# VectorE sums the squares of seven blocks for three RMS norms, and the ones product of TensorE takes that sum and the eighth block

## What is computed

```python
def rmsnorm(x, g):
    xf = x.astype(jnp.float32)
    y = xf * lax.rsqrt(jnp.mean(xf * xf, axis=-1, keepdims=True) + RMS_EPS)
    return (y * g.astype(jnp.float32)).astype(x.dtype)
...
            x = x + mix
            x = x + swiglu(rmsnorm(x, p['norm_ffn_even'][i]), p['ffn_w_gate'][i], p['ffn_w_up'][i], p['ffn_w_down'][i])
        else:
            mix, cb = conformer_conv(rmsnorm(x, p['norm_mix_odd'][i]), conf_bufs[i], p, i)
            new_conf_buf.append(cb)
            x = x + mix
            x = x + moe_swiglu(rmsnorm(x, p['norm_ffn_odd'][i]), p['moe_router'][i], p['moe_w_gate'][i],
                               p['moe_w_up'][i], p['moe_w_down'][i])
```

## Time and profile before

| | |
|---|---|
| median of 3 runs | 1404.65 us |
| lowest, highest | 1401.75 us, 1405.23 us |
| the profiled execution | 1402.96 us |
| its span, first to last instruction | 1401.2 us |
| mean granted clock of TensorE | 0.988 |
| TensorE busy | 1351.3 us (96%) |
| VectorE busy | 363.2 us (26%) |
| ScalarE busy | 178.7 us (13%) |
| GpSimd busy | 61.9 us (4%) |

### The profile page before, as it was taken

The page is one execution under the profiler, slowest core; times in us unless marked ns, Lnnn a source line. Parts: engine busy times, 40 slices in busy tenths (PEclk is TensorE's granted clock), DMA queues, the critical chain, the costliest instruction groups (busy, mean ns, idle before and its releaser), DMA issues.

```text
span 1401.2 us, 18234 instructions
## 1 busy us (share of the span) xinstructions
PE 1351.3 (96%) x7743; PEld 868.3 (62%) x7743; DVE 363.2 (26%) x807; ACT 178.7 (13%) x376; POOL 61.9 (4%) x87
## 2 busy tenths in 40 slices
PE   7999998999999999989999999999999999999976
PEld 6888887888888888758755544434343443444432
DVE  3536885221111006922300020201111011011102
ACT  1231423010001001041200000000000100100002
POOL 2004110000001002000000000000000000000000
PEclk9999999999999999999999999999999999999998
DMA  8538622574547233410899999999999999999994
GB/s 265 202 123 275 222 91 91 180 208 127 174 144 230 77 120 120 128 43 16 314 399 403 401 397 399 394 403 400 398 399 391 403 393 404 387 374 405 391 403 197
DMA packets 169667, 381.49 MB, mean 272 GB/s; under 512 B 7661, under 2 KB 63517, under 8 KB 169531
## 3 DMA queue, kind: packets, MB, share of 16 engines
q1 hardware_dynamic: 161571, 358.96, 69.2%
q0 software_dynamic: 3184, 11.40, 2.6%
q10 hardware_dynamic: 4834, 9.99, 2.2%
HBM read 372.41 MB, written 9.01 MB: 272 GB/s over the span
## 4 chain that ended last, share of the span: by engine, by line
PE 87%; DVE 6%; DMA 4%; SPq 1%; ACT 1%; issue 1%; ACTq 0%; DVEq 0%
PE ps L1703 29%; PE ps L2166 14%; PE ps L2231 12%; PE ps L2181 8%; PE ps L2191 4%; DVE region L1407 3%; PE ps L1921 3%; PE ps L2242 2%; PE ps L1712 2%; DMA region<-in_moe_w_gate_dram 2%; DMA big<-in_moe_w_down_dram 1%; PE ps L2123 1%; PE ps L2085 1%; DMA big<-in_w_in_even_dram 1%; PE ps L2208 1%
## 5 line engine op out<-in xcount | busy, mean ns | idle before, releaser
L1703 PE MATMUL ps<-big 128*128 128x264 f32 x1376 | 311.9, 388 | 2.3 <-DMA big<-in_w_in_even_dram 2.3
L1703 PEld LDWEIGHTS ps<-big 128*128 128x128 f32 x1376 | 262.1, 191 | 48.2 <-DMA big<-in_w_in_even_dram 2.5
L2166 PE MATMUL ps<-big,region 128*64 128x384 f32 (+3 forms) x1200 | 217.7, 459 | 7.6 <-DMA big<-in_moe_w_up_dram 4.6
L2166 PEld LDWEIGHTS ps<-big,region 128*64 128x64 f32 (+1 forms) x1200 | 115.4, 147 | 105.4 <-issue 61.5
L1703 PE MATMUL ps<-region,big 128*128 128x264 f32 x704 | 162.4, 391 | 3.7 <-ACT region L965 3.7
L2231 PE MATMUL ps<-big,region 128*64 128x512 f32 (+1 forms) x608 | 156.1, 604 | 2.2 <-DMA big<-in_moe_w_down_dram 1.6
L1703 PEld LDWEIGHTS ps<-region,big 128*128 128x128 f32 x704 | 135.2, 193 | 27.6 <-issue 4.1
L2181 PE MATMUL ps<-big,region 128*64 128x384 f32 (+1 forms) x720 | 111.0, 460 | 0.0
L2231 PEld LDWEIGHTS ps<-big,region 128*64 128x64 f32 (+1 forms) x608 | 50.1, 144 | 93.7 <-issue 90.0
L2181 PEld LDWEIGHTS ps<-big,region 128*64 128x64 f32 x720 | 51.3, 137 | 56.6 <-issue 49.0
L1618 DVE TENSOR_TENSOR region<-region,ps 128x384 f32<-128x384 f32 (+1 forms) x24 | 12.2, 520 | 227.0 <-PE ps L2166 227.0
(11 more groups left out here) (366 smaller groups left out, 1048.9 us busy)
## 6 DMA issues: line engine op xcount, KB each, us to landing
big<-in_moe_w_up_dram SPq DMA_DIRECT2D x48, 1536.0 KB
big<-in_moe_w_gate_dram SPq DMA_DIRECT2D x40, 1536.0 KB
big<-in_moe_w_down_dram SPq DMA_DIRECT2D x40, 1536.0 KB
big<-in_w_in_even_dram SPq DMA_DIRECT2D x10, 2048.0 KB
big<-in_moe_w_gate_dram SPq DMA_DIRECT2D x16, 1024.0 KB
big<-in_moe_w_up_dram SPq DMA_DIRECT2D x16, 1024.0 KB
big<-in_moe_w_down_dram SPq DMA_DIRECT2D x16, 1024.0 KB
region<-in_moe_w_gate_dram SPq DMA_DIRECT2D x8, 1536.0 KB
```

The lines of the kernel that those rows point to most:

```text
L1703: ins = mm(ps[:, 0:T], w[:, c, cols:cols + P], src[:, c, :], start=c == 0, stop=c == nk - 1)
L2166: ins = mm(out, xg[:, 4 * j + c, 0:cap], w[:, c, r, :], start=j + c == 0, stop=j + c == 4)
```

## The change

VectorE gets six adds per norm. Ahead of residual c, for c from 2 to 7, it waits until block c - 1 has been squared, and adds it to block 0 of `SQ2`. So block 0 ends as the sum of blocks 0 to 6. TensorE's products with ones behind the `wo`, `fd` and `w2` tiles are taken out. In place of the last one stands `stat_two`, with two products: the sum, and block 7.

```diff
             def residual(k, name, bias=None, gain=None):
 
                 for c in range(DC):
+                    if c >= 2:
+                        dve.wait_ge(sem("sq_ready"), 8 * (k + 1) + c)
+                        reach()
+                        ins = v.tensor_tensor(SQ2[:, 0, :], SQ2[:, 0, :], SQ2[:, c - 1, :], ALU.add)
+                        if c < DC - 1:
+                            after(ins)
+                        else:
+                            ins.then_inc(sem("sq_summed"), 1)
                     filled(dve, (name, c))
                     src = tile((name, c))[:, 0:T]
...
+            def stat_two(k):
+
+                pe.wait_ge(sem("stat_read"), STATS.index(f"norm{k}"))
+                pe.wait_ge(sem("sq_summed"), k)
+                mm(STAT[:, 0:T], ones[:, :], SQ2[:, 0, :], start=True, stop=False)
+                pe.wait_ge(sem("sq_ready"), 8 * k + DC)
+                mm(STAT[:, 0:T], ones[:, :], SQ2[:, DC - 1, :], start=False, stop=True).then_inc(sem("stat_full"), 1)
+
...
                 done(ins)
-                for c in range(AHEAD) if n == AHEAD else (n - 1,):
-                    stat("norm1", "sq_ready", 8, SQ2, c)
...
                         if s + j + m == 0:
-                            stat("norm1", "sq_ready", 8, SQ2, DC - 1)
+                            stat_two(1)
...
                     project(("fd", 2 * s + j), w, P * j, FC, HT)
-                    if 2 * s + j:
-                        stat("norm2", "sq_ready", 16, SQ2, 2 * s + j - 1)
...
                         if s + j + m == 0:
-                            stat("norm2", "sq_ready", 16, SQ2, DC - 1)
+                            stat_two(2)
...
                     project(("w2", 4 * s + j), w, P * j, DC, CC, ("cc_ready", 0) if s + j == 0 else None)
-                    if 4 * s + j:
-                        stat("norm3", "sq_ready", 24, SQ2, 4 * s + j - 1)
...
             turn_rows("ht", 0, HTK[0], H)
-            stat("norm3", "sq_ready", 24, SQ2, DC - 1)
+            stat_two(3)
```

## The result

The changed kernel takes 1394.91 us (median of 6 runs, 1388.73 to 1396.0), against 1403.92 us before (median of 6, 1401.75 to 1405.76). The ratio is 0.9931, with a 95% interval of 0.9917 to 0.9946: 9.7 us less, between 7.6 and 11.7 us. Forecast were 8.0 us, and 1396.6 us in a range of 1393.5 to 1400.5 us.

A forecast was written before the change was run, and what follows sets the result against it. It took an unbroken TensorE chain up to the first expert load, then an expert part set by its weight stream, as the bound. Median 1404.65 us, less 8.0 us for 18 products, adds free: 1396.6 us, range 1393.5 to 1400.5.

The forecast's parts named there:

- What bounds the kernel: Unbroken TensorE work at norms 1 to 3 sets the first expert load; the expert part's end moves with its start.
- microsecond or two: Expert part, first expert load to end: the forecast is wrong if its length changes by more than this.
- What is removed: Norms 1, 2 and 3: 18 products with ones go, 0.445 us each by the pitch, 8.0 us in all.
- The durations: Removed products priced by record duration, 386 ns a record: 13.9 us saved; left aside as counting overlap twice.
- the weight loads alone: Removed products priced at 190 ns of weight load a record: 6.8 us saved, time 1397.8 us.
- What is added: VectorE's 18 adds, 6.3 to 7.7 us, lie under projections at no cost; about 2.1 us left at `w2`.
- What is moved: The sum's product goes behind the `fg`, `cv` or row-turning work; TensorE issues as much between last residual tile and root.
- Rival B, spared: TensorE's clock fall at `w2`, 3.07 us lost on the path, is spared: 1393.5 us; chance 0.05.
- the clock rows at `w2` differ: Sign in the profile after: a different granted clock at `w2` would show the forecast wrong.
- Rival B, dearer: Second clock fall comes earlier, over the chain behind `w2` to the router: up to 3.9 us, 1400.5 us; chance 0.09.
- Rival C: VectorE's waits reach the path: 18 adds with their squares delay TensorE by 15.3 us, 1411.9 us; chance 0.03.
- Rival D: No change that can be told: saving lost ahead of the first expert load, or slower weight stream; chance 0.07.

The follow-up runs named there:

- before filled: Kernel before, with seven products with ones issued while TensorE waits for ScalarE ahead of `w2`: 1401.43 us, ratio 0.9985.
- one product a norm: Changed kernel with VectorE also adding block 7, leaving TensorE a single product with ones per norm: 1395.15 us, ratio 0.9942.
- the adds alone: Kernel before plus VectorE's 18 adds into a scratch tile nothing reads, all 24 products kept: 1405.23 us against 1405.13 us, ratio 0.9997.
- the filled kernels: Kernel before and changed kernel, each with seven products with ones in TensorE's wait ahead of `w2`: 1401.43 us; 1393.59 us, again 1392.64 us.

## Why the prediction was right

**What bounds the kernel: right.** Time added or removed ahead of the first expert load comes out at the end. The expert part was 730.26 to 733.54 us long in all twelve profiled executions, whether its start lay at 659.22 or at 703.66 us. It drifts by up to 3 us, more than the "microsecond or two" that I allowed. In five profiles (before, changed twice, before filled, one product a norm) the last load of expert weights in the chain takes 19.0 to 19.2 us and goes into `big`, and the part is 730.26 to 730.95 us; in the other seven the load takes 20.7 to 20.8 us and goes into `region`, and the part is 730.92 to 733.54 us. Why is open. When TensorE itself starts on the experts matters little: before, its first expert product at 678.87 us waited for VectorE's work behind the router, in the changed kernel the one at 671.76 us waited for its weights, and yet the part differs by only 0.7 us.

**What is removed: right.** The price was 0.445 us a product, from the pitch. Seven at `wo` gave 3.12 us, six at norm 3 gave 2.67 us, 72 more cost 31.90 us. The durations (13.9 us for 18) and the weight loads alone (6.8 us for 18, 27.4 us for 72) are both refuted. The Trainium skill (Perfetto Trace Analysis, Identifying the Most-Contended Engine) judges TensorE's room by two figures, the share of its peak arithmetic and the busy share of weight loads. Here the second is 85% in a stretch in which no product can be had for nothing; as a measure of room for one more product, it doesn't hold in this case. The first was not worked out.

**What is added: right.** The adds took 432 to 435 ns an add, which the row of line 1192 gave as 429 ns, and 2.14 us of room at `w2` where the working had about 2.1 us. Four more adds fit, eight do not.

**What is moved: right.** The first expert load was forecast for 662.2 us. It came at 663.54 us: 2.59 us late from the part ahead of the change, 1.15 us early from the clock, 0.14 us unexplained.

**Rival B, spared:** it happened in part, and so a sign came true that the prediction had named as speaking against its forecast, "the clock rows at `w2` differ". The loss at `w2` fell from 3.07 to 1.92 us (2.00 us in the second profile), and was 1.92 to 1.98 us in four other kernels, but 3.24 us with the adds alone and 3.02 us with one product a norm. The loss followed the granted clock of the first 7 us of `w2`: 0.57 to 0.60 in the three kernels that lost 3.02 to 3.24 us, 0.76 in both profiles of the changed kernel. But the removed products alone don't decide it: the kernel with each product four times lost 1.96 us, the one with one product a norm 3.02 us. Nor does the place of `w2` in time alone: that kernel began `w2` at 615.79 us, and the changed kernel's second profile, with 2.00 us, at 615.48 us. What sets it is open, since each kernel has one or two profiles; that it helped the changed kernel in both is luck as far as these runs show. The prediction priced it at 3.1 us; by the filled kernels 0.64 us of that is not the clock's. The Trainium skill (TensorE: Matmul & The Clock Gate, What's actually happening) says that lack of activity throttles the array's clock and activity releases it. The filled kernels agree, with a clock of 1.00 where TensorE no longer idles.

**Rival B, dearer: it did not happen here.** The chain from the last `w2` tile to the first expert load is 15.01 us against 15.11 us before, at a granted clock of 1.00 from 655 to 663.5 us. That it can is seen in two other kernels: behind its waits the one with eight more adds lost 3.15 us at a clock of 0.50 and then 0.76, and the kernel before filled lost 0.36 us.

**Rival C: refuted** as far as this change goes, and its edge found between four and eight more adds. **Rival D: refuted** by the fourfold products, and by the expert part of the changed kernel, no longer than before. The drift of up to 3 us in other profiles is of the size that it feared.

**The size.** The medians differ by 9.0 us where 8.0 us were forecast. The interval holds 8.0 us, and 1.15 us of clock would make up the rest; that the clock is the rest was seen in the profiles, and is not shown for the medians. The forecast time is 1.7 us above the measured one: 0.7 us of this is the median of before, 1403.92 us by six runs where the forecast stood on 1404.65 us by three, and 1.0 us is the size.

## What to carry to other kernels

On an unbroken chain of TensorE, as here, the price of a matmul is its pitch, from its own start in the chain to the start of the piece behind it, not the duration of its records. Work for a reduction over partitions can be summed by an idle VectorE first, block by block, as long as every tile leaves it time for residual, square and add; count that interval against the tile's pitch, and the rest costs nothing. Where a single profile is compared with another, cut both at an instruction ahead of the change and at one behind it, since the parts that nobody touched moved by up to 3 us here.

## What was not expected of the hardware

Waits of TensorE cost nearly twice their length: 3.92 us of waits were followed by a stretch at a granted clock of 0.50, and 7.5 us were lost in all. And the stretch ahead of the change, the same instructions in every kernel, ended anywhere from 251.30 to 254.27 us, with a granted clock from 90 to 150 us of 0.92 to 0.93 in the four profiles that came latest (253.29 us and later) and 0.98 to 1.00 in the eight others. That stretch isn't the whole cause: the kernel with one product a norm came at 253.27 us with a clock of 0.98 there.
